# One core, PE-bound: high-weight passes first, a reordered scan, one queue for the first loads, six key banks

## The reference

```python
# block 1, on 16 meta tokens + 256 tokens (T = 272)
h = concat([meta, x]);  xn = rms_norm(h, g_pre_mix)
b, c, hh, q, k, v, g_conv, g_attn = split(xn @ w_in)
y_conv = b * causal_dwconv(c * hh, conv_w_mix)
o = stick_breaking_attention(q, k, v)                  # 16 heads of 64
merged = sigmoid(g_conv) * (y_conv @ w_proj_conv) + sigmoid(g_attn) * (o @ w_proj_attn)
h = h + rms_norm(merged @ w_out)
u, g = split(rms_norm(h) @ w_up_gate)
h = h + rms_norm((gelu(causal_dwconv(u)) * g) @ w_down)
# block 2, layer 0: SSD scan (16 heads) beside gated linear attention, GLA (8 heads)
z, xbc, dt, q, k, v, gate, g = split(rms_norm(h) @ even_w_in)
y_a = rms_norm(ssd_chunked_scan(silu(conv(xbc)), dt) * silu(z))
o_b = rms_norm(gla_chunked(q, k, v, decay)) * silu(g)
h = h + concat([y_a, o_b]) @ even_w_out
# layer 1: softmax attention with an output gate, then the last norm
q, k, v, z = split(rms_norm(h) @ odd_w_in)
out = rms_norm(h + (attention(q, k, v) * silu(z)) @ odd_w_out)
```

## Time and profile before

| what | value |
|---|---|
| median of 3 runs | 846.91 us (846.84 to 847.1) |
| the profiled execution | 846.78 us |
| its span, first to last instruction | 844.9 us |
| mean granted TensorE clock | 0.998 |
| PE, PEld busy | 830.4 us, 799.7 us |
| DVE, ACT, POOL busy | 622.5, 504.9, 120.2 us |
| DMA from HBM | 137.65 MB, 164 GB/s over the span |
| chain that ended last, by engine | PE 82%, DVE 9%, ACT 5% |

### The profile page before, as it was taken

The page is one execution under the profiler, slowest core; times in us unless marked ns, Lnnn a source line. Parts: engine busy times, 40 slices in busy tenths (PEclk is TensorE's granted clock), DMA queues, the critical chain, the costliest instruction groups (busy, mean ns, idle before and its releaser), DMA issues.

```text
span 844.9 us, 16864 instructions
## 1 busy us (share of the span) xinstructions
PE 830.4 (98%) x6770; PEld 799.7 (95%) x6770; DVE 622.5 (74%) x1055; ACT 504.9 (60%) x876; POOL 120.2 (14%) x119
## 2 busy tenths in 40 slices
PE   8999999999999999999999999999999999999997
PEld 7999999999999999999999999998898999888896
DVE  6647888886666688677664488999797696568765
ACT  6346657555454576555554468797868555356655
POOL 1000000000000305433441100042414010000002
PEclk9999999999999999999999999999999999999999
DMA  8744435445555536655666535545444376654431
GB/s 307 254 153 141 154 104 173 128 138 175 187 181 193 173 101 193 196 188 179 195 194 187 192 101 166 176 153 184 149 152 153 114 229 183 191 169 136 125 101 50
DMA packets 39853, 139.81 MB, mean 165 GB/s; under 512 B 4432, under 2 KB 5088, under 8 KB 39648
## 3 DMA queue, kind: packets, MB, share of 16 engines
q1 hardware_dynamic: 37728, 135.22, 50.1%
q10 hardware_dynamic: 2048, 3.51, 1.3%
HBM read 137.65 MB, written 1.06 MB: 164 GB/s over the span
## 4 chain that ended last, share of the span: by engine, by line
PE 82%; DVE 9%; ACT 5%; issue 1%; DMA 1%; POOL 1%; SPq 0%; DVEq 0%; ACTq 0%; POOLq 0%
PE ps L1806 66%; PE ps L1834 4%; PE ps L1809 4%; DVE weights_lo L1077 3%; ACT weights_hi L549 1%; PE ps L1949 1%; PE ps L1934 1%; DMA raw_weights<-weights_in 1%; PE ps L1963 1%; PE ps L2217 1%; PE ps L2235 1%; DVE arena L1388 1%; PE ps L2225 1%; POOL arena L479 0%; ACT arena L888 0%
## 5 line engine op out<-in xcount | busy, mean ns | idle before, releaser
L1077 DVE TENSOR_TENSOR weights_lo<-raw_weights,weights_hi 128x1024 fp32r<-128x1024 f32 x251 | 311.8, 1247 | 87.1 <-ACT weights_hi L549 86.8
L1806 PE MATMUL ps<-x_hi,weights_hi 128*128 128x256 f32 (+3 forms) x1272 | 367.8, 289 | 1.2 <-DVE weights_lo L1077 0.5
L1806 PE MATMUL ps<-x_lo,weights_hi 128*128 128x256 f32 (+3 forms) x1272 | 358.1, 282 | 0.0
L1806 PE MATMUL ps<-x_hi,weights_lo 128*128 128x256 f32 (+3 forms) x1272 | 357.9, 281 | 0.0
L549 ACT ACTIVATE weights_hi<-raw_weights 128x1024 fp32r<-128x1024 f32 x251 | 263.2, 1053 | 147.6 <-PE ps L1806 61.0
L1806 PEld LDWEIGHTS ps<-x_hi,weights_hi 128*128 128x128 f32 x1272 | 239.2, 188 | 8.7 <-issue 6.0
L1806 PEld LDWEIGHTS ps<-x_lo,weights_hi 128*128 128x128 f32 x1272 | 239.6, 188 | 0.7 <-issue 0.5
L1806 PEld LDWEIGHTS ps<-x_hi,weights_lo 128*128 128x128 f32 x1272 | 239.5, 188 | 0.0
L1806 PE MATMUL ps<-y_hi,weights_hi 128*128 128x256 f32 (+1 forms) x488 | 137.7, 282 | 0.0
L1806 PE MATMUL ps<-y_lo,weights_hi 128*128 128x256 f32 (+1 forms) x488 | 137.4, 282 | 0.0
L1806 PE MATMUL ps<-y_hi,weights_lo 128*128 128x256 f32 (+1 forms) x488 | 137.1, 281 | 0.0
(11 more groups left out here) (268 smaller groups left out, 1069.9 us busy)
## 6 DMA issues: line engine op xcount, KB each, us to landing
raw_weights<-weights_in SPq DMA_DIRECT2D x251, 512.0 KB, 3.8
arena<-decay_rows ACTq DMA_DIRECT2D x8, 256.0 KB, 3.9
masks<-masks_in SPq DMA_DIRECT2D x1, 1186.0 KB, 7.1
raw_weights<-weights_in SPq DMA_DIRECT2D x4, 256.0 KB, 6.0
hidden<-xT_in SPq DMA_DIRECT2D x2, 272.0 KB, 6.7
hidden<-xT_in ACTq DMA_DIRECT2D x1, 276.0 KB, 4.0
hidden<-xT_in ACTq DMA_DIRECT2D x1, 272.0 KB, 5.9
gate_w<-gate_w_in ACTq DMA_DIRECT2D x1, 256.0 KB, 3.7
```

The costliest lines, as they stand in the source:

```text
L1077: d.sig(TT(wlo[:, s * CW:(s + 1) * CW], raw[:, (c % RAW) * CW:(c % RAW + 1) * CW], whi[:, s * CW:(s + 1) * CW].bitcast(F32), ALU.subtract) ...
L1806: ins = mm(bank(BANK_OF[no])[:, 0:b - a], wt, x_[:, kt, a:b], start=s0, stop=s1)
```

## The change

In words, part by part:

- `project` goes through a tile chunk by chunk: first both passes with high weights over all of the chunk's blocks, when `hi_ready`, then the low-weight pass over all of them, when `lo_ready`. The matmuls are the same in number and size.
- `first_keys` makes its passes as their parts arrive: high by high, then the low weights or low x, whichever is due.
- The keys `k 4` and `k 5` get PSUM banks 4 and 5 in place of 0 and 1.
- `first_total` stands at the last block of `k 3` in place of block 4. Five dummy matmuls in place of six.
- All first loads are issued by SP, half chunks and x in turn; `params` follows chunk 3.
- DVE, MLP: `ffn_conv(1)` ahead of `feed(fu 1)`.
- Scan, ACT: `take_keys(1)` ahead of `half_tanh(eg 2)`; in rounds 2 and 3 `feed(ev)` ahead of `gla_exps`.
- Scan, DVE: in rounds 2 and 3 `ssd_args(u)` ahead of `feed(eq)`; in round 1 `gla_states(1)` and `conv_in(ex 5)` right behind `feed(eg 3)`.

```diff
-OTHER_BANKS = {("fu", 2): (4,), ("fg", 2): (5,), ("ex", 1): (5,)}
+OTHER_BANKS = {("k", 4): (4,), ("k", 5): (5,), ("fu", 2): (4,), ("fg", 2): (5,), ("ex", 1): (5,)}
@@ SP
-            load_half(0, 0)
-            load_half(1, 0)
-            load_half(0, 1)
-            load_x(2)
-            load_half(1, 1)
-            load_x(3)
+            for n in range(4):
+                load_half(n % 2, n // 2)
+                load_x(n)
             for c in range(2, NCHUNKS):
                 if c == RAW:
+                    sp_.dma_start(prm[:], params).then_inc(S("load_params"), 16)
@@ ACT
-            for n in range(2):
-                w_ = slice(KT + 2 * n * T if n else 0, KT + 2 * n * T + 2 * T)
-                act.dma_start(first_x[:, w_], xT[:, w_]).then_inc(S(f"load_x{n}"), 16)
-            act.dma_start(prm[:], params).then_inc(S("load_params"), 16)
@@ ACT, scan, p > 1
                     gla_squares(p - 1)
+                    feed(("ev", p))
                     gla_exps(p)
-                    feed(("ev", p))
                     take_values(p)
@@
                 feed(("eg", u))
+                if p == 1:
+                    take_keys(1)
                 half_tanh(("eg", u), gs[:, u % 4, :])
@@
                 feed(("ez", u + 1))
-                if p == 1:
-                    take_keys(1)
@@ DVE, MLP
+            ffn_conv(1)
             feed(("fu", 1))
-            ffn_conv(1)
@@ DVE, scan, p > 1
+                    ssd_args(u)
                     feed(("eq", p))
                     z_full(("ex", u + 1), xs[:, u + 1, :], name="xsilu")
-                    ssd_args(u)
@@ DVE, scan
                 feed(("eg", u + 1))
+                if p == 1:
+                    gla_states(1)
+                    conv_in(("ex", 5))
                 z_full(("ez", u + 1), zs[:, 1, :])
@@
                 if p == 1:
                     decay_sums(1)
-                if p < 3:
-                    conv_in(("ex", u + 3))
-                gla_states(p)
+                else:
+                    if p < 3:
+                        conv_in(("ex", u + 3))
+                    gla_states(p)
@@ PE, project
+                j0 = 0
+                while j0 < nb:
+                    c = (f + j0) // BPC
+                    j1 = min(nb, (c + 1) * BPC - f)
+                    for w_, parts, signal in ((whi, (hi, lo), "hi_ready"), (wlo, (hi,), "lo_ready")):
+                        pe.wait_ge(S(signal), c + 1)
+                        for j in range(j0, j1, step):
+                            kt, at = j // step, (c % RING) * CW + ((f + j) % BPC) * P
+                            if w_ is whi and ready is not None:
+                                ready(kt)
@@ PE
-            for _ in range(6):
+            for _ in range(5):
                 mm(bank(6)[:, 0:L], aw[:, 0, 0:P], aw[:, 0, 0:L], start=True, stop=True)
@@ PE, first_keys
                 for n in range(4):
                     for c in range(2):
+                        if n % 2 == 0:
+                            pe.wait_ge(S("hi_ready" if n else "hi_half"), c + 1)
+                        part(c, n, whi, xhi, "x_hi")
+                        if n % 2 == 0:
+                            if c:
+                                part(c, n, whi, xlo, "x_split")
+                            pe.wait_ge(S("lo_ready" if n else "lo_half"), c + 1)
+                        part(c, n, wlo, xhi, "x_hi")
+                        if n % 2 == 0 and c == 0:
+                            part(c, n, whi, xlo, "x_split")
+                    if n % 2:
+                        for c in range(2):
+                            part(c, n, whi, xlo, "x_split", n == 3)
             def first_total(kt):
-                if kt == 4:
+                if kt == KT - 1:
                     pe.wait_ge(S("load_masks"), 16)
                     total(1, 0)
```

More of the change, by code:

```diff
@@ L401, in load_x @@
             def load_x(n):
-                w_ = slice(KT + 2 * n * T, KT + 2 * n * T + 2 * T)
+                w_ = slice(KT + 2 * n * T if n else 0, KT + 2 * n * T + 2 * T)
                 sp_.dma_start(first_x[:, w_], xT[:, w_]).then_inc(S(f"load_x{n}"), 16)
@@ L1791, in project @@
                 step = 1 if toks is None else nb // KT
-                for j in range(0, nb, step):
-                    c, kt = (f + j) // BPC, j // step
-                    at = (c % RING) * CW + ((f + j) % BPC) * P
-                    if (f + j) % BPC == 0 or j == 0:
-                        pe.wait_ge(S("lo_ready"), c + 1)
-                    if ready is not None:
-                        ready(kt)
-                    first, last = j == 0, j + step >= nb
-                    outs = [None] if toks is None else toks
-                    for o, tok in enumerate(outs):
-                        for n, (w_, x_) in enumerate(((whi, hi), (whi, lo), (wlo, hi))):
-                            wt = w_[:, at:at + step * P]
-                            s0, s1 = first and n == 0, last and n == 2
-                            if tok is None:
-                                ins = mm(bank(BANK_OF[no])[:, 0:b - a], wt, x_[:, kt, a:b], start=s0, stop=s1)
-                            else:
-                                t0, t1 = tok
-                                ins = mm(bank(BANK_OF[no + o])[0:t1 - t0, 0:step * P], x_[:, kt, t0:t1], wt,
-                                         start=s0, stop=s1)
-                        if last:
-                            ins.then_inc(S("out_ready"), 1)
-                    if (f + j + step) % BPC == 0 and not last:
@@ new lines, in project @@
+                outs = [None] if toks is None else toks
+                j0 = 0
[8 more added lines that the diff above has]
+                                ready(kt)
+                            first, last = j == 0 and w_ is whi, j + step >= nb and w_ is wlo
+                            wt = w_[:, at:at + step * P]
+                            for o, tok in enumerate(outs):
+                                for m, part in enumerate(parts):
+                                    s0 = first and m == 0
+                                    if tok is None:
+                                        ins = mm(bank(BANK_OF[no])[:, 0:b - a], wt, part[:, kt, a:b],
+                                                 start=s0, stop=last)
+                                    else:
+                                        t0, t1 = tok
+                                        ins = mm(bank(BANK_OF[no + o])[0:t1 - t0, 0:step * P], part[:, kt, t0:t1], wt,
+                                                 start=s0, stop=last)
+                                if last:
+                                    ins.then_inc(S("out_ready"), 1)
+                    if j1 < nb:
@@ L1814, in project @@
                         ins.then_inc(S("chunk_read"), 1)
+                    j0 = j1
             def project_together(tiles, hi, lo, spans, ready_hi, ready_lo, after=None):
@@ L1881, in _, with part @@
             pe.wait_ge(S("zeroed"), 1)
-            for _ in range(6):
+            for _ in range(5):
                 mm(bank(6)[:, 0:L], aw[:, 0, 0:P], aw[:, 0, 0:L], start=True, stop=True)
             def first_keys():
+                def part(c, n, w_, x_, ready, stop=False):
+                    no = FIRST_OUT["k", c]
+                    for kt in (2 * n, 2 * n + 1):
+                        pe.wait_ge(S(ready), kt + 1)
+                        ins = mm(bank(BANK_OF[no])[:, 0:T], w_[:, c * CW + kt * P:c * CW + kt * P + P], x_[:, kt, 0:T],
+                                 start=kt == 0 and w_ is whi and x_ is xhi, stop=stop and kt == 2 * n + 1)
+                    if stop:
+                        ins.then_inc(S("out_ready"), 1)
@@ L1887, in first_keys @@
                 for n in range(4):
                     for c in range(2):
-                        no = FIRST_OUT["k", c]
-                        if n == 0:
-                            pe.wait_ge(S("lo_half"), c + 1)
-                        if n == 2:
-                            pe.wait_ge(S("lo_ready"), c + 1)
-                        for kt in (2 * n, 2 * n + 1):
-                            pe.wait_ge(S("x_split"), kt + 1)
-                            at = c * CW + kt * P
-                            for k, (w_, x_) in enumerate(((whi, xhi), (whi, xlo), (wlo, xhi))):
-                                ins = mm(bank(BANK_OF[no])[:, 0:T], w_[:, at:at + P], x_[:, kt, 0:T],
-                                         start=kt == 0 and k == 0, stop=kt == KT - 1 and k == 2)
```

2 lines of the change are left out of this document (removed).

## The result

The changed kernel took 849.78 us (median, 849.02 to 850.09), the one before 846.86 us in the same session: a ratio of 1.0032, 95% interval 1.0023 to 1.0042. It is slower by 2.9 us; that is 0.3 us above the wide range of the prediction (844.2 to 849.5) and 0.9 above its own one (846.4 to 848.9). The profiled execution, the slowest of the seven, took 850.09 us with a span of 848.0, 3.1 us more than before. In later sessions four executions, two of the kernel before and two of one experiment, took some 2834 us; the medians leave them out.

The account below looks back on a forecast made before the run. PE bounds the kernel, busy 830.4 of 844.9 us, so only its gaps were priced: -1.55 + 0.1 + 0.63 + 0.1 - 0.5 + 2.05 = +0.83 us, giving 847.7 us; own range 846.4 to 848.9, wide range 844.2 to 849.5.

Parts of the forecast that it names:

- The start: First keys: chunk 2 lands 0.6 us sooner, the tree ends at 17.56, k 4 starts at 19.3, 1.55 us earlier (0.6 to 2.3).
- a sign of being wrong: Start of k 4: the forecast is wrong if it moves by less than 0.6 us.
- one queue is slower: Rival, first loads: ten DMAs in a row on SP, the start gains nothing, 849.3 us; chance 0.16.
- The pace: Dense stretches of PE: second semaphore wait of each tile costs nothing, 0 to 1 us over 251 chunks.
- The scan: Rounds 2 and 3: PE's removed waits return, ACT idles 1.8 us before the second split of ev 3; +2.05 us (-1.0 to +2.6).
- the sign that I gave: Scan's end: the eight matmuls of ssd_heads(7) would take 3 to 4 us.
- mk 0: Tile mk 0: block 7 is asked for earlier, so PE waits for the last low block of x; +0.63 us (0.4 to 0.8).
- ex 0: Tile ex 0: next tile about 0.55 us later, nearly all taken back by following waits on DVE; net +0.1 us.
- The MLP: MLP's start: ffn_conv(1) earlier removes PE's waits at 323.45 and 326.86, less 0.57 of fg 1; -0.5 us (0 to -1.0).
- The cold start: Rival, PE's first passes: one dummy less, the clock may rise later; +1.2 us, 848.9 us; chance 0.10.
- the attention layer: Tile mq 1: scores are asked for after 4 passes, not 6; +0.1 us.

Follow-up runs that it names:

- the kernel without the wait at `gla_out(2)`: Kernel with all the helpful edits (844.80 us), plus gla_states ahead of the gating and conv_in in round 2 too: 845.15 us, ratio 0.998 to the kernel before.
- The swap: Kernel before with only ffn_conv(1) moved ahead of feed(fu 1) on DVE: 846.55 us, ratio 0.9995.
- the three orders that are slow from 39 to 275 us: Kernel before with only project's pass order and its waits changed (high parts first, 848.06 us), or only the order: pairs of blocks (848.13), runs of eight (848.51).
- pairs: Kernel before, waits unchanged, passes reordered per two blocks as four high-weight then two low-weight, except in block-by-block tiles: 848.13 us, ratio 1.0015.
- The kernel with a wait of 1.98 us for POOL: Helpful edits together, gla_states ahead of the gating in round 2, plus gla_rms(1) ahead of gla_exps(2) and take_values(2): 846.60 us, ratio 1.0000.

## Why the prediction was wrong, point by point

- **The start failed**, as the step "chunk 2 has about 0.1 MB less ahead of it ... I take 0.6 us ... so the tree ends at 17.56". Measured: chunk 2 taken at 11.90, not 10.8; the tree ended at 18.66. Behind it all followed my working: from the total to `k 4` I had 1.72 us, it was 1.78, and `k 4` came 0.25 earlier in place of 1.55, less than the 0.6 that I had named as a sign of being wrong. The error was to give the order of the queue a gain in the last arrival, for which the earlier trace rows had no price but an average of transfers; the rival "one queue is slower" had that mechanism right. In size the rival went too far the other way, with no gain at all at the start. The gain that was to be had on the tree lay in DVE's own order, in the timeline from which the earlier trace rows are taken: between the additions of the tree stands a split of 1.22 us.

```profile
14.49 1.29 DVE L1120 TENSOR_TENSOR arena<-arena 128x1088 f32<-128x1088 f32 x1 [0.78 <-ACT arena L604]
15.70 1.22 DVE L1077 TENSOR_TENSOR weights_lo<-raw_weights,weights_hi 128x1024 fp32r<-128x1024 f32 x1
16.96 0.73 DVE L1124 TENSOR_TENSOR arena<-arena 128x544 f32<-128x544 f32 x1
```

- **The pace failed**, as "The second semaphore wait of each tile I cost at nothing", with 0 to 1 us as its bounds. Nothing was right for the wait. But the edit also changes which passes follow one another, and this I did not price at all. It cost 0.8 us up to 275 (1438 matmuls in the 170 us instead of 1443). I had written that 0.001 us a matmul would be 6 us, and put no rival on it.
- **The scan was right** in its mechanism: waits of 1.5 us at `turn_keys(2)` and 1.2 at `gla_out(2)`, ACT idle for 1.75 us, +2.10 for +2.05. Two details were off. `take_values` came 2.23 us later (640.60 for 638.37); my own terms give 2.13 and not 2.05. And the sign that I gave, eight matmuls that take 3 to 4 us, did not come: they took 1.91, and the loss stood in front of them (1.41) and at `turn_keys(3)` (1.03), which I had not named. What took PE's lead away in round 2 is the chain of ACT and DVE: confirmed by the kernel without the wait at `gla_out(2)`, in which the wait only moved.
- **`mk 0` was right**: 0.75 for 0.63, of which 0.45 is the wait in the trace; the 0.3 beyond it I take for the refill of the array, which no run here isolates. `ex 0` cost 0.28 instead of 0.1, and such a term is missing from its sum too.
- **The MLP** came out at -0.55 for -0.5 by luck, not by the edit that I credited. High parts first alone removed both waits (-0.56 in the kernel with `project` alone changed). The swap showed a gain, of 0.39, in the kernel with the old order.
- **The cold start** did not happen: PE's first passes run 0.125 apart from 5.65 us on, wherever none of them waits for data.
- The range was too narrow because it took the rivals one at a time. With the start's rival and the 0.8 of the pace, inside its bound of 1 us, it is 847.7 + 1.55 + 0.8 = 850.05. That this comes so near to the 850.09 of the profiled execution is in part luck: the start lost 1.1 of the 1.55, and another 0.4 came from `ex 0`, `mk 0` and the attention layer (0.18, 0.12 and 0.08 above my terms).

## What to carry to other kernels

Where PE is full, a new order of its passes is an edit of its own, to be priced over all tiles: count the matmuls of a dense stretch in both traces, since neither the busy share nor the waits show it, and do it in several stages, since the sign can change. A wait removed from the full engine is worth something only if the engines that feed it have slack behind it; follow their chain to its next meeting with PE before adding the gain. For a start that hangs on a reduction, look between the steps of the reduction before looking at the transfers.

## What the runs showed of the hardware

- **A wait that is met is free.** One more in nearly every tile: 1443 matmuls in 170 us, as before.
- **The order of passes changes the pace.** With high parts first PE's shift grows by 0.43 us from 75 to 191 us, over some 30 tiles of 24 passes with 258 or 260 columns, 15 ns a tile; from 39 to 75 us, mostly tiles of 272 columns, it ends where it began, at -0.19 (-0.26 in between). In the three orders that are slow from 39 to 275 us the three products of a block are taken apart, but how much each loses differs from stage to stage, and pairs gain 0.46 us from 705 to 726. What in the engine makes the difference no run here shows; it stays open.
- **A long wait can cost the clock.** In the kernel of the 2.00 us wait, stretch, PE busy (x), clock, DMA share, GB/s, ahead of and behind it:

```profile
620.00:630.00 10.00, 10.00 (x93) 1.00 0.50 154
...
640.00:644.00 4.00, 4.00 (x24) 0.58 0.48 158
644.00:648.00 4.00, 4.00 (x37) 1.00 0.42 131
```

From 640.8 to 644.0 us the passes stand 0.21 us apart instead of 0.12: the lower level of 1.2 GHz, entered 1.1 us after the work had begun again. Sixteen passes at 0.1 are 1.5 us. The kernel with a wait of 1.98 us for POOL has the same in its trace, 0.9 us behind the wait. The traces with waits of up to 1.6 us don't have it. It did not happen in every execution, to judge by the mean granted clock of each: 0.996 in three of ten in that kernel, which took 1.1 to 1.8 us longer than the rest. Each kernel has a trace of one execution only, so for the others this is an inference. The waits of 1.58, 1.24 and 0.46 us cost less than nearly the same time in two (1.54 and 2.00). The Trainium skill (TensorE: Matmul & The Clock Gate, What's actually happening) has the gate closed by default and released by activity; the trace agrees: behind the idle 2.0 us the lower level came, and it went while PE worked.
